# Hybrid decoder layer on one core: order of the routing work ahead of the first experts

## What is computed

```python
h = rmsnorm(x, norm_mix); proj = h @ w_in
...                                     # state-space branch, window attention, gates, output projection
x = x + merged @ w_out
h2 = rmsnorm(x, norm_ffn)               # 512 tokens x 1024
g = top-1 of 4 groups (h2 @ w_coarse);  pick top-2 of its 4 experts (h2 @ w_fine)
gates[token, expert] = softmax(top 2) * g_prob
gu = einsum('nd,edf->nef', h2, w_up)    # 16 experts, 1024 -> 2*256
act = silu(gu[..:256]) * gu[256:] * gates
out = x + einsum('nef,efd->nd', act, w_down)
```

## Time and profile before

| | us |
|---|---|
| median of three runs | 585.73 |
| the profiled execution, its own time | 585.89 |
| its span, first to last instruction | 584.1 |
| PE busy | 529.7 (91%) |
| DVE busy | 387.8 (66%) |
| ACT busy | 282.8 (48%) |
| POOL busy | 161.1 (28%) |
| scatters into the output (L656), 16 | 31.2 busy on POOL, 81.2 idle in front of them |
| low part of the up weights (L1465), 24 into one of two places | 55.0 busy, 2292 ns each |

### The profile page before, as it was taken

How to read it: one execution, slowest core, us unless ns; L and a number is a source line. 1 busy time by engine, 2 the same in 40 slices (tenths; PEclk the granted TensorE clock), 3 DMA queues, 4 the chain that set the end, 5 groups by cost and what they waited for, 6 DMA issues and landing times.

```text
span 584.1 us, 7461 instructions
## 1 busy us (share of the span) xinstructions
PE 529.7 (91%) x2634; PEld 426.2 (73%) x2634; DVE 387.8 (66%) x648; ACT 282.8 (48%) x460; POOL 161.1 (28%) x344
## 2 busy tenths in 40 slices
PE   1699899998999998989999899957799999999982
PEld 1589787886786786777888788956678877777761
DVE  3984485874874974856665733466789887878740
ACT  4616126435445445474234401233477677878741
POOL 2241227098095095000000000020223222233122
PEclk9999999999999999999999999966899999999997
DMA  8723620220120111013256837427999999986422
GB/s 306 132 74 109 180 73 1 73 73 15 58 72 9 64 55 36 20 55 108 72 175 241 297 135 289 184 104 283 409 390 331 332 338 340 325 297 203 136 41 35
DMA packets 62326, 94.46 MB, mean 162 GB/s; under 512 B 13873, under 2 KB 45649, under 8 KB 62289
## 3 DMA queue, kind: packets, MB, share of 16 engines
q1 hardware_dynamic: 56288, 80.84, 40.2%
q0 software_dynamic: 4608, 8.40, 6.3%
q10 hardware_dynamic: 1392, 4.74, 2.0%
HBM read 88.71 MB, written 12.58 MB: 173 GB/s over the span
## 4 chain that ended last, share of the span: by engine, by line
PE 56%; DMA 26%; DVE 9%; ACT 4%; issue 3%; POOL 0%; ACTq 0%; POOLq 0%; DVEq 0%
DMA out_dram<-arena_back,idx_all 21%; PE pj L1582 10%; PE pj L1584 10%; PE pj L1583 10%; PE sc L1659 3%; DMA arena_front<-h_rows,idx_all 3%; DVE split L411 2%; PE m L1716 2%; PE sc L1658 2%; DMA arena_back<-in_norm_mix_dram 1%; PE tp L1668 1%; PE sc L1810 1%; DMA arena_front<-in_w_in_dram 1%; ACT arena_back L808 1%; PE m L1582 1%
## 5 line engine op out<-in xcount | busy, mean ns | idle before, releaser
L1582 PE MATMUL pj<-h_high,split 128*128 128x512 f32 x192 | 77.7, 405 | 2.3 <-DVE h_low L1051 2.3
L1584 PE MATMUL pj<-h_high,split 128*128 128x512 f32 x192 | 75.6, 394 | 0.0
L1583 PE MATMUL pj<-h_low,split 128*128 128x512 f32 x192 | 75.5, 393 | 0.0
L1465 DVE TENSOR_TENSOR up_low<-arena_front,up_high 128x2048 fp32r<-128x2048 f32 x24 | 55.0, 2292 | 12.3 <-ACT up_high L887 12.2
L1928 PE MATMUL pj<-up_high,xt_high 128*128 128x512 f32 x128 | 51.6, 403 | 2.9 <-DVE xt_low L1497 2.9
L656 POOL DMA_INDIRECT out_dram<-arena_back,idx_all x16 | 31.2, 1951 | 81.2 <-DMA out_dram<-arena_back,idx_all 62.2
L569 POOL TENSOR_TENSOR rstd<-ssq,half_col 128x1 f32<-128x1 f32 x8 | 6.4, 797 | 165.5 <-DVE ssq L1002 153.9
L887 ACT ACTIVATE up_high<-arena_front 128x2048 fp32r<-128x2048 f32 x24 | 46.1, 1926 | 11.8 <-PE pj L1930 11.0
L1929 PE MATMUL pj<-up_low,xt_high 128*128 128x512 f32 x128 | 50.9, 398 | 0.0
L1930 PE MATMUL pj<-up_high,xt_low 128*128 128x512 f32 x128 | 50.8, 397 | 0.0
L411 DVE TENSOR_TENSOR split<-arena_front,split 128x2048 fp32r<-128x2048 f32 (+1 forms) x21 | 44.6, 2124 | 6.1 <-ACT split L404 5.2
(11 more groups left out here) (335 smaller groups left out, 1312.6 us busy)
## 6 DMA issues: line engine op xcount, KB each, us to landing
arena_front<-in_w_expert_up_dram SPq DMA_DIRECT2D x24, 1024.0 KB, 18.2
arena_back<-in_w_expert_down_dram SPq DMA_DIRECT2D x16, 1024.0 KB, 16.5
arena_front<-in_w_in_dram SPq DMA_DIRECT2D x13, 1024.0 KB, 5.5
arena_back<-in_w_expert_up_dram SPq DMA_DIRECT2D x8, 1024.0 KB, 18.9
arena_front<-in_w_out_dram SPq DMA_DIRECT2D x4, 1024.0 KB, 5.3
arena_back<-in_x_dram SPq DMA_DIRECT2D x4, 512.0 KB, 5.0
arena_front<-in_w_ssm_glu_gate_dram SPq DMA_DIRECT2D x8, 256.0 KB, 2.8
arena_front<-in_w_ssm_glu_val_dram SPq DMA_DIRECT2D x8, 256.0 KB, 3.3
```

What stands on the lines that cost most here:

```text
L1465: tt(up_low[i % NH][:], ring[i % NH], up_high[i % 3][:].bitcast(F32), ALU.subtract).then_inc(up_low_done, 1)
L1582: pe.matmul(dst, sh, mh, start=first and i == 0, stop=False)
L1583: pe.matmul(dst, sh, ml, start=False, stop=False)
L1584: ins = pe.matmul(dst, sl, mh, start=False, stop=last and i == len(terms) - 1)
```

## The change

VectorE computes the shares directly after the indices of experts 0 and 1, and the low part of the first weight half after them. It makes the selections of lists 2 and 3 there, and reads these lists after the low part of expert 0's rows. PE places lists 2 and 3 after turning expert 0's rows, ahead of its products. The remaining pairs move one step forward: step e places the pair of lists 2(e+2) and 2(e+2)+1, for e from 0 to 5. In `up`, the one wait for all of the turned rows becomes a wait for each half, ahead of blocks 0 and 4.

```diff
             for e in range(2):
                 v.wait_ge(idx_full, e + 1)
                 ts(idx_all[:, e:e + 1], sc[e][:, 128:129], ...).then_inc(first_idx, 1)
-            low_up(0, 0)
             v.wait_ge(r_act, 1)
...
             tt(tg[:, :, :, 3], share, tg[:, :, :, 2].bitcast(F32), ALU.subtract).then_inc(shares_done, 1)
+            low_up(0, 0)
+            for e in range(LISTS[1], LISTS[2]):
+                pick_list(e)
             v.wait_ge(idx_full, 3)
...
             low_rows(0)
+            read_lists(1)
             low_up(0, 1)
             for e in range(NE):
-                if 1 <= e <= LAST_LISTS + 1:
-                    read_lists(e)
-                if e <= LAST_LISTS:
-                    for n in range(LISTS[e + 1], LISTS[e + 2]):
+                if 1 <= e <= LAST_LISTS:
+                    read_lists(e + 1)
+                if e < LAST_LISTS:
+                    for n in range(LISTS[e + 2], LISTS[e + 3]):
                         pick_list(n)
...
             def up(e, ks):
-                pe.wait_ge(xt_done, (e + 1) * 2)
...
                 for k in ks:
+                    if k % (DC // 2) == 0:
+                        pe.wait_ge(xt_done, e * 2 + 1 + k // (DC // 2))
...
             place_shares()
             turn_rows(0)
+            pe.wait_ge(idx_done, 1)
+            place_lists(LISTS[1], LISTS[2])
             for e in range(NE - 1):
                 up(e, range(DC))
-                if e <= LAST_LISTS:
-                    pe.wait_ge(idx_done, e + 1)
-                    place_lists(LISTS[e + 1], LISTS[e + 2])
+                if e < LAST_LISTS:
+                    pe.wait_ge(idx_done, e + 2)
+                    place_lists(LISTS[e + 2], LISTS[e + 3])
```

## The result

The changed kernel takes 585.99 us in the median of 20 runs (579.99 to 591.81), the kernel before 588.88 in the median of 20 runs beside it (584.61 to 593.77). The ratio is 0.9929 [0.9906, 0.9953], so 4.2 us faster (2.8 to 5.5), which is under 1%, about what a measurement of this kernel can tell from no change. That ratio is not the quotient of the two medians: these differ by 2.9 us, which lies inside the same interval. Forecast were 6.4 us and 579.5. Of the 6.5 us between 579.5 and 585.99, 3.15 are the base: the three runs shown had their median at 585.73, the twenty at 588.88. The rest is gain that did not come: 2.2 us by the ratio, 3.3 by the medians. The measured time lies outside the range, 576.5 to 584.0.

A forecast was written before the change was run, and what follows sets the result against it. From 440.5 us on, only the serial scatters were taken to bound the kernel. Expert 0's down projection ending at 421.3 instead of 427.76 gave 6.4 us, passed on whole: 585.89 - 6.4 = 579.5, range 576.5 to 584.0.

The forecast's parts named there:

- the gather: Expert 0's gather on GpSimd: with shares first, 1.0 to 1.3 us instead of 3.19, landing 2.0 us sooner.
- rival A: The 3.19 us of expert 0's gather on GpSimd are its own; end 580.7 to 582.1 us; chance 0.20.
- the 6.0: Gain in us if VectorE's share operations stood until the gather's descriptors are written, rows turned at 396.2 instead of 395.8.
- the clock: PE's full clock back at 401 us, expert 0's products ending 405.9; a fall charged before expert 1's, ending 416.0.
- the stall and the first links: Expert 2's gather issued about 401 us, its 1.80 us stall gone; scatter 0 issued at 423.6, scatter 1 at 434.
- To the end: All scatters move 6.4 us; the loads' end moves too, so 0 charged for one more long scatter of 2.9.
- the 136 us: Sign of failure: scatters 2 to 15 taking longer in sum than the 136 us between 440.48 and 576.34.
- B: Rival: DMA engines, full in this stage, give gain back; 1.5 to 4.3 us left, end 581.6 to 584.4; chance 0.19.
- C: Rival: slower; expert 2's gather shares the weight-load burst, everything behind 5.7 us later, end 591.6; chance 0.04.
- D: Rival: an unseen wait, lists before second low part, holds PE as long; within 1.5 us of 585.9; chance 0.04.
- T1: Follow-up theory, not the prediction's: a few down weights come late behind up weights in SyncE's queue; bytes are no limit.
- T3: Follow-up theory, not the prediction's: the DMA engines' total bounds the stage; loads end when they end, whoever runs ahead.

The follow-up runs named there:

- b2_shares: Kernel before with only the shares moved ahead of the first weights' low part; ratio 0.9977 to the kernel before.
- a3_lowfirst: Changed kernel with the first weights' low part back ahead of the shares; ratio 0.998 to the kernel before.
- second profile: Profile of the changed kernel run again with nothing altered; ratio 0.9925 to the kernel before.
- a4_thindown: Changed kernel loading half of each down weight of experts 8 to 15, 4 MB less; ratio 0.9852 to the kernel before.
- a5_early2: Changed kernel with two weight-half loads (2 MB) issued ahead of the wait for the h2 stores; ratio 0.9961 to the kernel before.
- a6_early4: Changed kernel with four weight-half loads (4 MB) issued ahead of the wait for the h2 stores; ratio 0.9922 to the kernel before.
- a7_stores2: Changed kernel with two weight-half loads issued behind the h2 stores but ahead of gather 0; ratio 0.9904 to the kernel before.
- a1_held: Changed kernel with each up weight half issued two releases later on SyncE; ratio 0.9927 to the kernel before.
- a9_downq: Changed kernel with down weights 4 to 15 issued from ScalarE's queue instead of SyncE's; ratio 0.999 to the kernel before.

## Why the prediction was partly right

*Right: the gather.* 1.0 to 1.3 us was taken for gather 0 on POOL and 1.29 came; rival A (3.19 its own) is out, by this and by b2_shares and a3_lowfirst, which move the 3.19 with the low part. The rule of the Trainium skill (SBUF — State Buffer, Who interferes with whom) would have held the share operations until about 396.98; they ran at 396.01 and 396.42. For POOL as the second comer the trace agrees once more (3.09 at 397.28); so the 6.4 and not the 6.0 was the sum to take.

*Right in sum, wrong in two terms: the clock.* "The clock was back 3.3 us after PE took up work", and from it "I take 401", failed: expert 0's products took 8.6 us and not 6.25, which is 1.9 us at their end, since they began 0.5 sooner than forecast. Uninterrupted work of transposes and small placings from 400.24 did not bring the clock back as I had assumed; it came at 409.3. "1.53 cost it the clock the last time, so I charge it again" failed the other way: the idle 0.93 brought no fall. The products of expert 1 thus began 1.4 us sooner for 3.2 forecast, and ended 2.8 for 3.0. The two misses cancel, and the 6.3 at the down projection is part luck.

*Right: the stall and the first links.* Gather 2 was issued at 404.75, which is 400.4 on the clock of the trace before, where 401 was said. Scatter 0 at 423.7 on that clock for 423.6, scatter 1 at 434.5 for 434.

*Wrong: "To the end".* The step reads: "If the loads' end did not move, one more scatter would be long: 2.9. Loads are issued as PE frees their places, so the end moves too; I charge 0." The first sentence is what happened in the first profile, to 0.05 us: scatter 11 is followed after 9.90 instead of 7.05. The second is false: the loads' end did not move with PE, so the term was not 0. Against the forecast 6.4 it came to 2.9 us in one profile and 2.6 in the other. A DMA share of 0.97 and 1.02 stood in my own rows, and should have made me doubt that a load issued sooner lands sooner. After the change the share is 1.00 to 1.03 from 404 to 480 in the windows, the up weights' median landing went from 18.4 to 21.6 us and the down weights' from 16.5 to 23.0, and the loads' end stayed (158.5, 158.7; 158.9 in the second profile). The runs that moved it (bytes: a4_thindown; start: a5_early2, a6_early4, a7_stores2) brought compute back to 142.8 us from scatter 0 on.

*Missed: the tightest weight.* I had read the landing of up weights, whose reserve is large, and not set each down weight's landing against its use. One row would have shown 1.8 us at 540.35. Experts 6 to 7 us ahead had to wait there. The prediction's own marker for this, scatters 2 to 15 "longer in sum than the 136 us", fires: 138.3.

*The rivals.* B, at 0.19, is the one that happened, by its first price: a long scatter more, 1.5 to 4.3 us left; 4.2 by the ratio, 3.5 and 3.8 in the two profiles. It lacked the late weights. In the second profile it is the whole of the path: the scatters alone hold the end. C did not come about: gather 2, in the burst, was there before PE wanted it. D is out, at the front at least, where 6.3 us came. The range in us was missed because of the base as well: as a gain on its own base it ran from 1.9 to 9.4 us, which holds 4.2 and 2.9. Twenty runs of the same kernel spread over 9 us, and three of them are a poor base for a range of 7.5.

*What stays open.* Whether the long scatters or the late weights cost more is not separated in the total time; in one profile the weights hold the end, in the other the scatters. T1 was not tested by itself: a1_held left the order of the loads alone, and a9_downq made the scatters longer. T3 is not exact either: behind 480 us the DMA share after is 0.87, 0.94 and 0.85 in stretches of 20 us, and the last down weights are issued only when PE frees their buffers (the last at 140.8 us after the index). The equal ends of 158.5 and 158.7 are thus in part chance; the equal landings up to expert 12 are the better evidence. Why the parts' totals sum to less than the whole, and a5_early2's ratio, are not explained. A kernel with fewer bytes changes the number of loads' packets and their time together; which of the two counts was not tried.

## What to carry to other kernels

Where a stage's DMA share is near 1, loads may land at the same moments however much sooner they are issued, as here up to expert 12; compute that is moved ahead of them is then paid back at the tightest load. Before charging nothing for "the loads move too", list landing against use for every load of every kind and take the least reserve: 1.8 us here, for a gain of 6.3. Dropping bytes let the gain through (0.9852, with half the down weights of eight experts left out). Starting bytes earlier took the late weights away, but no gain in total time was told from the changed kernel's. A second queue took here from what was serial.

## What the runs showed of the hardware

- The granted clock stayed at 0.5, the 1.2 GHz level, while PE worked on without a gap from 400.24: transposes, placings of 4 columns, and then 5.7 us of dense products, until 409.3 (0.56 in 407 to 410, 1.00 behind). After 0.93 us idle at 414.95 it did not fall (1.00 in 413 to 416), where after 1.53 us idle before it had (0.80 for the product at 412.00, 0.50 us for the one at 414.95).
- The spread of 1.5 to 2% between runs of one kernel goes with the mean clock, though not strictly: the changed kernel's run of 579.99 us had a mean granted clock of 0.974, its run of 586.66 had 0.964, that of 591.81 had 0.959, but so had one of 586.02. A part lies in stretches that the change does not touch (0.94 against 1.00 in 200 to 255).
- Twelve 1 MB loads moved from one hardware queue to a second shortened the down weights' landing from 23.0 (all sixteen) to 11.1 us in the median, lengthened the up weights' from 21.6 to 28.5 and stretched the scatters' spacing from about 10 to about 12 us, with the same bytes.
- Loads that were issued up to 7 us sooner in the full stage landed at the same moments (109.9 and 109.7, 147.4 and 147.4 us after the index), and single issue instructions of SyncE, 0.37 us at the shortest, took as much as 6.61 us before and 9.04 after.
- An indirect DMA that starts on POOL just behind the start of a subtraction of two SBUF inputs on DVE held POOL for 3.09, 3.59 (at 521.81) and 3.65 us, instead of 1.0 to 1.6. The price moves with the subtraction. POOL paid it as the second comer; DVE as the second comer did not (396.01 and 396.42 inside gather 0, and 430.04).
